# Block transposes on VectorE and 32x32 score tiles in the paged attention of a decoder step

## The chip, the cores and the metric

One NeuronCore of a Trainium2 chip runs the whole program. The metric is the device time of one launch in microseconds (us), as the median of several runs. The core has TensorE (PE, matmuls), VectorE (DVE), ScalarE (ACT), GpSimd (POOL) and SyncE (SP, which here only issues DMAs), and sixteen DMA engines that they share. Each engine works through its own queue in order and waits on semaphores. SBUF and PSUM have 128 partitions; PSUM has eight banks of 512 f32 columns.

## What is computed

One inference step of a hybrid decoder layer: a prompt of 1024 tokens and eight samples of eight new tokens each, with shared weights. The part that the change touches is the samples' attention over a paged cache. Each sample has eight pages of 128 past keys and values; a page of keys is 128 x (8 heads x 128) f32, 512 KB, of values the same. Each head's 128 channels are two components of 64, and the two softmaxes are subtracted.

```python
def sample_attention(q, k_new, v_new, lam, k_cache, v_cache, page_table, layer):
    k_past = k_cache[layer, page_table].reshape(b, -1, N_HEADS, 2, HEAD_DIM)
    v_past = v_cache[layer, page_table].reshape(b, -1, N_HEADS, V_DIM)
    s_past = jnp.einsum('bqhcd,bkhcd->bhcqk', q, k_past, preferred_element_type=jnp.float32)
    s_new = jnp.einsum('bqhcd,bkhcd->bhcqk', q, k_new, preferred_element_type=jnp.float32)
    s_new = jnp.where(jnp.tril(jnp.ones((t, t), dtype=bool)), s_new, NEG)
    s = jnp.concatenate([s_past, s_new], axis=-1) * scale
    p = diff_probs(s, lam).astype(v_new.dtype)      # softmax of component 0 - lam * softmax of component 1
    return (jnp.einsum('bhqk,bkhe->bqhe', p[..., :n_past], v_past)
            + jnp.einsum('bhqk,bkhe->bqhe', p[..., n_past:], v_new))
```

Around it stand the input projection (q, k, v, a pooling input u and two gates), prompt attention, a pooling mixer, the merge of both branches and a gated channel mixer.

## The kernel before

The program has five phases, each engine's part written out by hand in one function per phase (`pe_phase2`, `act_phase2` and so on), with counted semaphores between. Nothing is scheduled by a tool: the order of the code is the order on each engine.

**Phase 1** projects q, k and v head by head and does the prompt's attention of head h beside the projection of head h+1. `pe_head` has nine steps s; a step has scores (`pe_scores`, L338), a projection piece, transposes of the probabilities (`pe_probs_transpose`, L351) and the values. VectorE's part is `dve_head`: in step s first `dve_probs` of step s-1 (L672 to L675), then `dve_max` (L663 to L665), and in step 1 also the scaling L656. The last head has no next projection; in its place stand nine **chunks** (`pe_chunk`, L1011) of the gates' projection. A chunk is one 128-column weight tile against 384 (or, the last of three, 320) tokens, 8 x 3 matmuls, since each product is split in three for precision. There are 14 weight tiles, 42 chunks.

**Phase 2** is the paged part. It goes in 32 turns of two key pages, and five more for the values that lag behind. Per key page TensorE makes eight 128x128 transposes into two PSUM banks (`pe_key_page`, L1068), ScalarE copies them out (`act_key_page`, L1181, `ktp`), and `pe_page_scores` (L1083) makes eight matmuls: the 32 stationary columns of a head are its 8 queries x 2 components beside zeros (`q_blk`, filled by `pool_queries`, L1268), so four heads' results lie in four groups of 32 partitions. `pe_new_scores` (L1093) does the same for the new keys. When a sample's eight pages are done, `dve_keys` takes the maximum, `act_sample_exp` the exponentials (`es`), and `dve_keys` makes the matrix `pick_r`, with which `pe_probs` (L1101, L1107) transposes, normalises and subtracts the probabilities in one matmul per page. `dve_pages` (L1246, L1248) copies them to SBUF (`pts`), and `pe_value_page` (L1126) multiplies them with the values (`v_pg`), five turns later. In nearly every turn stands one of the remaining 33 chunks.

Keys have a ring of four pages (`RK`), values one of five (`RV`); the last two value pages go to key slots. SP loads them page by page (`sp_load_page`, L1296), reading the page's number from SBUF first, in one queue with the weight tiles (`fm_load`, L1470, one raw buffer, waits until POOL has split the tile before). Gate results of the first six tiles stay in SBUF (`sig_p`), the other eight go to DRAM from a ring of two rows (`act_spill`, L1036) and come back in phase 3. Before phase 2's first keys SP does this, in order:

```python
            for g in range(2):
                sp_load_keys(e, g)
            sp_store_kv(e, NH - 1, 1)
            e.wait_ge(b7_free, b_use(NH - 2, True, ("o", TT - 1)) + 1)
            e.wait_ge(kv_st[0], NH // 2 * 64 + 1)
            for g in range(2, RK):
                sp_load_keys(e, g)
```

`sp_store_kv` waits for the last head's keys to have their gain (POOL, L781), since they share SBUF with it. `phase1_over` waits until the last head's outputs are stored.

## Time and profile before

| | us |
|---|---|
| median of 3 runs | 2083.44 |
| lowest, highest | 2081.55, 2084.08 |
| profiled execution: its span | 2081.0 |
| phase 2, first key transpose (551.0) to last value page (825.2) | 274.2 |
| TensorE busy | 2073.9 |
| VectorE, ScalarE, GpSimd busy | 1045.5, 677.1, 493.4 |

A row of the timeline has the start, the duration, the engine, the source line, the operation with what it writes and reads, and how many instructions were merged. Matmuls are pipelined: a row's duration holds the pipe's end, so what a piece costs is read from its start to the next one's start. An f32 matmul shows as two records.

### The profile page before, as it was taken

What the parts mean: (1) busy time and instruction counts of PE and PEld (TensorE: products, weight loads), DVE (VectorE), ACT (ScalarE), POOL (GpSimd) and SP (SyncE); (2) the same over time, 40 slices, a digit from 0 to 9 for tenths busy, and PEclk for the clock granted to TensorE, in tenths of its full rate; (3) what the DMA queues carried; (4) which work ended last, traced back from release to release, by engine and by line L of the source; (5) the groups of instructions that cost most, each with busy time, mean ns of one, the idle gap of its engine ahead of it and who ended that gap; (6) DMA issues with size and microseconds to landing.
All of it is one profiled execution on the core that took longest, in us unless ns stands there. A gap on an engine that the chain in (4) does not pass through costs nothing.

```text
span 2081.0 us, 34047 instructions
## 1 busy us (share of the span) xinstructions
PE 2073.9 (100%) x13497; PEld 1904.7 (92%) x13497; DVE 1045.5 (50%) x1400; ACT 677.1 (33%) x1328; POOL 493.4 (24%) x358
## 2 busy tenths in 40 slices
PE   9999999999999999999999999999999999999999
PEld 8888888888898998999999989999899999899997
DVE  6766666665311111466553433555555455555556
ACT  5444445444444442225112322221131122113120
POOL 5333333332111011332322011221221122022110
PEclk9999999999999999999999999999999999999999
DMA  5222212122388887212224500110111111112112
GB/s 152 58 63 58 62 41 57 32 63 78 102 269 274 309 302 246 59 37 68 83 90 135 166 11 31 51 46 28 53 60 32 42 51 42 32 53 60 32 41 98
DMA packets 174545, 185.53 MB, mean 89 GB/s; under 512 B 8240, under 2 KB 147260, under 8 KB 174404
## 3 DMA queue, kind: packets, MB, share of 16 engines
q1 hardware_dynamic: 162588, 174.10, 26.8%
q10 hardware_dynamic: 11824, 9.51, 1.4%
q8 instruction: 102, 1.67, 0.3%
q14 instruction: 31, 0.25, 0.0%
HBM read 160.57 MB, written 23.24 MB: 88 GB/s over the span
## 4 chain that ended last, share of the span: by engine, by line
PE 99%; DVE 0%; ACT 0%; issue 0%; POOL 0%; POOLq 0%; DVEq 0%
PE PS L1498 39%; PE PS L2260 13%; PE PS L1011 8%; PE PS L2015 5%; PE PS L282 4%; PE PS L284 4%; PE PS L283 4%; PE PS L338 4%; PE PS L362 3%; PE PS L1068 3%; PE PS L351 2%; PE PS L1083 2%; PE PS L1126 2%; PE PS L1519 1%; PE PS L1531 1%; PE PS L317 1%
## 5 line engine op out<-in xcount | busy, mean ns | idle before, releaser
L1485 POOL TENSOR_TENSOR fw_lo<-fw_raw,fw_hi 128x1024 fp32r<-128x1024 f32 x86 | 215.9, 2510 | 876.5 <-ACT fw_hi L1481 876.5
L1498 PE MATMUL PS<-m_hi,fw_hi 128*128 128x384 f32 (+1 forms) x1032 | 228.2, 329 | 0.0
L1498 PE MATMUL PS<-m_lo,fw_hi 128*128 128x384 f32 (+1 forms) x1032 | 227.5, 328 | 0.0
L1498 PE MATMUL PS<-m_hi,fw_lo 128*128 128x384 f32 (+1 forms) x1032 | 227.4, 328 | 0.0
L2388 DVE TENSOR_TENSOR x<-x,PS 128x512 f32<-128x512 f32 x198 | 136.2, 688 | 142.2 <-PE PS L2260 142.0
L1498 PEld LDWEIGHTS PS<-m_hi,fw_lo 128*128 128x128 f32 x1032 | 176.3, 188 | 0.0
L1498 PEld LDWEIGHTS PS<-m_lo,fw_hi 128*128 128x128 f32 x1032 | 176.3, 188 | 0.0
L1498 PEld LDWEIGHTS PS<-m_hi,fw_hi 128*128 128x128 f32 x1032 | 176.0, 188 | 0.2
L282 PE MATMUL PS<-w_hi,act_hi 128*128 128x384 f32 (+1 forms) x456 | 164.7, 361 | 0.0
L284 PE MATMUL PS<-w_hi,act_lo 128*128 128x384 f32 (+1 forms) x456 | 153.6, 337 | 0.0
L283 PE MATMUL PS<-w_lo,act_hi 128*128 128x384 f32 (+1 forms) x456 | 153.1, 336 | 0.0
L2260 PE MATMUL PS<-wd_hi,f_hi 128*128 128x512 f32 x360 | 143.8, 399 | 0.1
L2260 PE MATMUL PS<-wd_lo,f_hi 128*128 128x512 f32 x360 | 142.0, 394 | 0.0
L1481 ACT ACTIVATE fw_hi<-fw_raw 128x1024 fp32r<-128x1024 f32 x86 | 91.3, 1061 | 150.1 <-DMA fw_raw<-in_w_up_dram 73.2
L2260 PE MATMUL PS<-wd_hi,f_lo 128*128 128x512 f32 x320 | 126.2, 395 | 0.0
L1011 PE MATMUL PS<-act_hi,fw_hi 128*128 128x384 f32 (+1 forms) x336 | 114.1, 340 | 0.0
L1181 ACT ACTIVATE ktp<-PS 128x512 f32<-128x512 f32 x128 | 69.6, 596 | 133.8 <-PE PS L1068 133.8
L1011 PE MATMUL PS<-act_hi,fw_lo 128*128 128x384 f32 (+1 forms) x336 | 109.7, 327 | 0.0
L1011 PE MATMUL PS<-act_lo,fw_hi 128*128 128x384 f32 (+1 forms) x336 | 109.6, 326 | 0.0
L2309 ACT ACTIVATE f_c<-f_c 128x1104 f32<-128x1104 f32 x22 | 24.6, 1120 | 255.2 <-DVE f_c L2362 255.1
L496 ACT ACTIVATE E<-PS,negm 128x256 f32<-128x256 f32 (+7 forms) x128 | 93.8, 740 | 26.4 <-DVE negm L665 25.4
L282 PEld LDWEIGHTS PS<-w_hi,act_hi 128*128 128x128 f32 (+1 forms) x456 | 85.3, 187 | 14.7 <-ACT raw L468 5.8
(317 smaller groups left out, 4254.7 us busy)
## 6 DMA issues: line engine op xcount, KB each, us to landing
k_pg<-in_cache_k_dram SPq DMA_DIRECT2D x64, 512.0 KB, 5.0
v_pg<-in_cache_v_dram SPq DMA_DIRECT2D x62, 512.0 KB, 5.2
fw_raw<-in_w_up_dram SPq DMA_DIRECT2D x44, 512.0 KB, 4.0
fw_raw<-in_w_in_dram SPq DMA_DIRECT2D x24, 512.0 KB, 4.5
wd_raw<-in_w_down_dram SPq DMA_DIRECT2D x22, 512.0 KB, 4.7
w_raw<-in_w_in_dram SPq DMA_DIRECT2D x21, 512.0 KB, 5.3
out_dram<-raw SPq DMA_DIRECT2D x16, 512.0 KB, 3.8
ga_scratch<-ga_ring ACTq DMA_DIRECT2D x8, 544.0 KB, 7.1
```

What stands on the lines that cost most here:

```text
L282: e.matmul(out, a_hi, h3, start=kt == 0, stop=False)
L283: e.matmul(out, a_hi, l3, start=False, stop=False)
L284: ins = e.matmul(out, a_lo, h3, start=False, stop=s < QT and kt == KT - 1)
L338: ins = e.matmul(PS[:, 2 * c + b // 512, 0:w], qT[slot][c * HD:(c + 1) * HD, s * P:(s + 1) * P], kT[slot][c * HD:(c + 1) * HD, b:b + w], s ...
L496: ins = e.activation(E[s % 2][:, c, 0:n], scores_ps[:, c, 0:n], ACT.Exp, bias=negm[:, s % 2, c:c + 1], scale=SCALE, accum_out=den[:, s % 2 ...
L1011: ins = e.matmul(PS[:, PJ + use % 2, 0:cw], w[n % 2][:, kt, :], x[:, kt, c0:c0 + cw], start=first and kt == 0, stop=last and kt == KT - 1)
L1481: e.activation(fw_hi[slot][:, 0:kts, :], fw_raw[:, 0:kts, :], ACT.Copy).then_inc(fw_head, 1)
L1485: e.tensor_tensor(fw_lo[slot][:, 0:kts, :], fw_raw[:, 0:kts, :], fw_hi[slot][:, 0:kts, :].bitcast(F32), ALU.subtract).then_inc(fw_tail, 1)
L1498: ins = e.matmul(PS[:, 3 * slot + c, 0:cw], w[slot][:, kt, :], x[:, kt, c0:c0 + cw], start=first and kt == 0, stop=last and kt == KT - 1)
L2015: ins = e.matmul(wo_banks(t)[:, half, :], a, w[:, half * 512:(half + 1) * 512], start=start, stop=stop)
L2260: ins = e.matmul(PS[:, bank, :], a, w[:, half * 512:(half + 1) * 512], start=first and k == 0, stop=last and k == 1)
L2388: ins = e.tensor_tensor(v, v, PS[:, bank, :], ALU.add)
```

## The change

Keys are no longer transposed by TensorE. A page lands in `k_ring`, one tensor of twelve slots, and VectorE transposes it in place in 32x32 blocks (`dve_turn_keys`): the channels of a block then lie in the 32 partitions that held its keys. Scores contract over 32 channels at a time. The queries must therefore lie in all four partition groups: SP writes them to DRAM (`q_dram`) and reads them back four times (`sp_load_queries`), and POOL spreads them in `q_blk` for one sample at a time. A sample's scores are one block of work, 32 matmuls of 64 columns for the new keys and 128 of 256 columns for the eight pages, each on one of 16 tiles of 32x32. Row group i writes bank i, four channel blocks and two heads of a pair accumulate. The columns come out in another order, which `act_sample_exp` puts right. VectorE sums the new scores over four banks first.

TensorE then has per sample: scores, two chunks, probabilities, four value pages, a chunk, four value pages and the new values, a chunk. One chunk stands ahead of the first sample. The last sample's values go to freed key slots. `es` has one buffer. Of the gate results only four tiles stay (`SIG_KEPT`); ten go to DRAM from one row `ga_row` in three pieces each, and two of them come back to `sig_p` at the start of phase 3. Seven key pages fit ahead of phase 2's memory (`KEYS_EARLY`), and VectorE turns six of them in the last head of phase 1.

```diff
@@ dve_head
+                if not proj and 1 <= s <= KEYS_TURNED_EARLY:
+                    dve_turn_keys(e, s - 1)
@@ memory
+        SIG_KEPT = 4
+        KEY_GROUP = NPG // 2
+        RK = 3 * KEY_GROUP
+        KEYS_EARLY = (raw_at[1] - R3 - SIG_KEPT * fit(TOK)) // fit(NH * VD)
+        KEYS_TURNED_EARLY = KEYS_EARLY // 2 * 2
+        k_ld = [sem(f"k_ld{j}") for j in range(RK // 2)]
@@ TensorE
+            e.wait_ge(k_turned, (b + 1) * NPG)
+            for r in range(2):
+                for x in range(XB):
+                    for i in range(4):
+                        part = slice(i * QB, (i + 1) * QB)
+                        for g in range(HG):
+                            c = (2 * g + r) * VD + x * QB
+                            ins = e.matmul(PS[g * QB:(g + 1) * QB, B_S + i, 0:2 * P], queries(g, r, x, part),
+                                           pages[part, :, :, c:c + QB], start=r == 0 and x == 0, stop=r == 1 and x == XB - 1)
+            ins.then_inc(sc_full, 1)
@@ pe_phase2
+            pe_chunk(e, P_FIRST, {})
+            for b in range(NB):
+                fill = [lambda p=p: pe_chunk(e, p, {}) for p in chunks_of(b)]
+                pe_scores_of_sample(e, b)
+                fill[0]()
+                fill[1]()
+                pe_probs(e, b)
+                for j in range(KEY_GROUP):
                     pe_value_page(e, b, j)
+                fill[2]()
+                for j in range(KEY_GROUP, NPG + 1):
+                    pe_value_page(e, b, j)
+                fill[3]()
@@ VectorE
+        def dve_turn_keys(e, g):
+
+            e.wait_ge(k_ld[g % RK // 2], 32 * (g // RK + 1))
+            page = k_ring[:, g % RK, :]
+            e.transpose(page, page).then_inc(k_turned, 1)
@@ SP
-            for g in range(2, RK):
+            for g in range(KEYS_EARLY):
                 sp_load_keys(e, g)
+            e.wait_ge(b7_free, b_use(NH - 1, False, ("k", 2)) + 1)
+            for b in range(NB):
+                e.dma_start(q_dram[:, b, :, :], qT_s[:, :, b * NS:(b + 1) * NS]).then_inc(q_st, 16)
+            e.wait_ge(q_st, 16 * NB)
+            for b in range(2):
+                sp_load_queries(e, b)
             for p in range(TT):
                 sp_chunk(e, p)
+            phase1_over(e)
+            sp_load_keys(e, KEYS_EARLY)
+            for g in range(2, RV):
+                sp_load_values(e, g)
+            for g in range(KEYS_EARLY + 1, RK):
+                sp_load_keys(e, g)
@@ SP, per sample
+                e.wait_ge(sc_full, b + 1)
+                for g in range(RK + b * NPG, RK + b * NPG + KEY_GROUP):
...
+                for k in range(NPG):
+                    if k == KEY_GROUP:
+                        sp_chunk(e, fill[2])
+                    if b * NPG + k + RV < (NB - 1) * NPG:
+                        sp_load_values(e, b * NPG + k + RV)
```

TensorE before, in a turn of phase 2 (a chunk stands ahead of these rows and behind them): transposes of a key page to PSUM, scores of the page before it from `ktp`, two value pages, scores, the next transposes.

```order
L1068 MATMUL PS<-ident,k_pg_103 128x128 x8
L1083 MATMUL PS<-ktp_113,q_blk_106 32x128 x4
L1083 MATMUL PS<-ktp_114,q_blk_106 32x128 x4
L1126 MATMUL PS<-v_pg_108,pts_121 16x256 x4
L1126 MATMUL PS<-v_pg_109,pts_121 16x256 x4
L1083 MATMUL PS<-ktp_115,q_blk_106 32x128 x4
L1083 MATMUL PS<-ktp_116,q_blk_106 32x128 x4
L1068 MATMUL PS<-ident,k_pg_104 128x128 x8
```

TensorE now, in the first sample: all scores in one piece (the first two rows), and after two chunks the probabilities with four value pages right behind them.

```order
L1089 MATMUL PS<-kT_s_53,q_blk_107 32x64 x32
L1098 MATMUL PS<-k_ring_102,q_blk_107 32x256 x128
...
L1106 MATMUL PS<-pick_r0_103,es_112 128x64 x8
L1112 MATMUL PS<-pick_r0_103,es_112 128x64
L1131 MATMUL PS<-v_pg0_123,pts0_113 16x256 x4
L1131 MATMUL PS<-v_pg1_124,pts0_113 16x256 x4
L1131 MATMUL PS<-v_pg2_108,pts0_113 16x256 x4
L1131 MATMUL PS<-v_pg3_109,pts0_113 16x256 x4
```

The transposes are gone from TensorE, and no chunk stands between a sample's probabilities and its values any more.

VectorE before, in step 1 of phase 1's last head: the end of `dve_max`, the scaling, and the four instructions of step 1's probabilities.

```order
L665 TENSOR_SCALAR negm_63<-row_max_62 128x2
L656 TENSOR_TENSOR raw1_81<-raw1_81,rs_61 128x3x256
L672 RECIPROCAL rden_65<-den_64 128x2
L673 TENSOR_SCALAR E1_87<-E1_87,rden_65 128x256
L674 TENSOR_SCALAR rden_65<-rden_65,neglam_66 128x1
L675 SCALAR_TENSOR_TENSOR E1_87<-E1_87,rden_65 128x256
```

VectorE now, at the same place.

```order
L665 TENSOR_SCALAR negm_63<-row_max_62 128x2
L656 TENSOR_TENSOR raw1_81<-raw1_81,rs_61 128x3x256
L1227 STREAM_TRANSPOSE k_ring_102<-k_ring_102 128x1024
L672 RECIPROCAL rden_65<-den_64 128x2
L673 TENSOR_SCALAR E1_87<-E1_87,rden_65 128x256
L674 TENSOR_SCALAR rden_65<-rden_65,neglam_66 128x1
```

The turn of the first key page, with its wait for the page's load, stands ahead of the step's probabilities; five more follow, one in each of the next steps.

## Rows read from the trace of the kernel before

**Rows 1.** The page: busy time of each engine, and the chain by engine.
```profile
PE 2073.9 (100%) x13497; PEld 1904.7 (92%) x13497; DVE 1045.5 (50%) x1400; ACT 677.1 (33%) x1328; POOL 493.4 (24%) x358
...
PE 99%; DVE 0%; ACT 0%; issue 0%; POOL 0%; POOLq 0%; DVEq 0%
```

**Rows 2.** Phase 2: window, PE, PEld, DVE, ACT, POOL busy, clock, DMA share, GB/s.
```profile
551.00:825.40 274.40, 274.40 (x3180) 245.46 (x3178) 33.05 (x93) 108.13 (x211) 30.61 (x39) 1.00 0.83 278
679.00:711.00 32.00, 32.00 (x385) 28.70 (x384) 3.23 (x10) 11.99 (x23) 2.86 (x3) 1.00 0.93 322
676.00:684.00 8.00, 8.00 (x95) 7.02 (x94) 1.69 (x8) 4.14 (x10) 0.00 (x0) 1.00 0.99 378
```

**Rows 3.** Timeline of TensorE in phase 2: start, duration, engine, line, what, records.
```profile
638.52 0.39 PE L1011 MATMUL PS<-act_hi,fw_hi 128*128 128x320 f32 x1
...
642.12 1.04 PE L1068 MATMUL PS<-ident,k_pg 128*128 128x128 f32 x8
643.09 0.65 PE L1083 MATMUL PS<-ktp,q_blk 128*32 128x128 f32 x16
...
643.77 1.05 PE L1126 MATMUL PS<-v_pg,pts 128*16 128x256 f32 x16
644.63 0.62 PE L1083 MATMUL PS<-ktp,q_blk 128*32 128x128 f32 x16
...
646.03 0.42 PE L1011 MATMUL PS<-act_hi,fw_hi 128*128 128x384 f32 x1
...
650.28 1.04 PE L1068 MATMUL PS<-ident,k_pg 128*128 128x128 f32 x8
...
654.48 1.90 PE L1101 MATMUL PS<-pick_r,es 128*128 128x64 f32 x16
...
656.41 0.42 PE L1011 MATMUL PS<-act_hi,fw_hi 128*128 128x384 f32 x1
```

**Rows 4.** Timeline of TensorE, last head: scores on two row halves.
```profile
528.32 1.78 PE L338 MATMUL PS<-kT,qT 64*128 64x512 f32 x8
```

**Rows 5.** The new keys' scores of one sample: duration, first and last start.
```profile
L1093 PE MATMUL PS<-kT_s,q_blk x16: 219/219/219, 643.5 to 643.7; 128*32 128x64 f32 x16
```

**Rows 6.** Timelines of VectorE, SP and TensorE early in the last head.
```profile
498.24 0.95 DVE L656 TENSOR_TENSOR raw<-raw,rs 128x768 f32<-128x768 f32 x1
...
503.37 0.68 SPq L881 DMA_DIRECT2D out_dram<-raw  x1
505.53 1.51 SPq L1296 DMA_DIRECT2D k_pg<-in_cache_k_dram  x2
...
503.40 0.38 PE L351 MATMUL PS<-ident,E 128*128 128x128 f32 x2
```

**Rows 7.** DMA to landing: two keys from 505.5, last outputs (551.6), eight spills.
```profile
DMA to landing us min/median/max: 3.7/4.2/4.7
...
DMA to landing us min/median/max: 2.3/2.3/2.3
...
DMA to landing us min/median/max: 2.7/7.1/8.0
```

**Rows 8.** Timeline of the last sample, from maximum to copied probabilities.
```profile
805.80 1.23 DVE L1230 TENSOR_REDUCE smax<-PS 128x1 f32<-128x1024 f32 x1 [0.65 <-PE PS L1083]
...
809.85 0.25 DVE L1241 TENSOR_SCALAR pick_r<-pick,sden 128x64 f32<-128x64 f32 x1
...
812.97 0.39 PE L1107 MATMUL PS<-pick_r,es 128*128 128x64 f32 x2
...
813.78 0.21 DVE L1248 COPY pts<-PS 128x64 f32<-128x64 f32 x1
```

**Rows 9.** Timeline of TensorE at the program's start.
```profile
8.35 1.91 PE L255 MATMUL PS<-ident,xt 128*128 128x128 f32 x8
...
11.03 0.52 PE L301 MATMUL PS<-w_hi,act_hi 128*128 128x384 f32 x1
...
13.46 0.33 PE L301 MATMUL PS<-w_hi,act_hi 128*128 128x384 f32 x1
```

More of the change, by code:

```diff
@@ L1088, in pe_new_scores, with key_groups @@
[L1088 to L1095 removed]
+        def key_groups(b):
+            first, second = 2 * b % 3, (2 * b + 1) % 3
+            return min(first, second), max(first, second), first > second
@@ L1786, in dve_phase3 @@
             e.tensor_copy(pre[:, 4 * P:4 * P + 3 * P // 2], PS[:, 7, PREP7:PREP7 + 3 * P // 2]).then_inc(prep_done, 1)
[L1787 to L1788 removed]
+            for c in range(NC):
+                e.wait_ge(ga_st[c], 16 * N_SPILLED)
             for m in range(KT):
```

370 lines of the change are left out of this document (154 added, 216 removed).

## The prediction

> **What bounds the kernel now.** I read three views in this order. The page's busy shares and its chain come first: TensorE is busy for 2073.9 of 2081.0 us and 99% of the chain is its own work [rows 1]. So a microsecond leaves the time only if TensorE issues less, and every new wait of TensorE adds in full. The windows come second [rows 2]: the paged part of the program (first key page at 551.0, last value page at about 825.2) takes 274.2 us, with the DMA engines 83% busy on average, 93% over 32 us in its middle, and 99% at 378 GB/s at their fullest. The second resource is therefore close behind the first. The third is TensorE's timeline inside that part [rows 3], which gives what each piece takes from its start to the start of the next.
>
> From [rows 3]: eight key transposes of a page 0.97 us (642.12 to 643.09); a page's eight score matmuls and the new keys' scores 0.68 (to 643.77), of which the new ones are 0.22 [rows 5]; two value pages 0.86 (to 644.63), so 0.43 each; scores and transposes of one more page 1.40 (to 646.03); the nine probability matmuls 1.93 (654.48 to 656.41); a projection chunk 4.25 at 384 columns (646.03 to 650.28) and 3.60 at 320 (638.52 to 642.12). Check: a key page is (0.97 + 0.46 + 1.40) / 2 = 1.42 and 64 are 91; new scores 2, 72 value pages 31, probabilities 15.5, and 33 chunks x 4.03 = 133 make 272.5 against 274.2.
>
> **The change part by part.**
>
> 1. TensorE's key work goes. Per sample that is 8 x 1.42 + 0.2 = 11.6 us. In its place stand 32 matmuls of 64 columns and 128 of 256 columns, each two records in the trace (before, a page's eight score matmuls show as x16 [rows 3]). Now tiles. Four column tiles run side by side before: 16 records of two value pages at 256 columns take 0.86 us, 4 x 0.215 [rows 3], so a record streams for 0.215 us and four share it. Two row tiles do as well: of the eight records of 64-row scores at 528.32, each half of the rows has two of 512 and two of 384 columns, 2 x (0.43 + 0.32) = 1.5 us, and all eight take 1.78 with the pipe's end [rows 4]; the halves in turn would take 3.0. Sixteen tiles are not in the trace. If all run side by side, 256 records / 16 x 0.215 = 3.45 us. If only two row tiles do, 6.9; if rows go in turn, 13.8. Issuing is no bound: sixteen records start within 0.2 us [rows 5], 14 ns each, so 16 in 0.22, a stream's length. I take 3.45, plus 0.45 for the new scores' 64 records at the closest issue seen and 0.2 for the change of tiling: 4.1 us per sample. Saved: 7.5 us x 8 = 60.
>
> The page "TensorE: Matmul & The Clock Gate" of the Trainium skill (section "Wait — 56ns, not 53.3ns?") speaks against this: starts never come closer than about 25 ns. By it the sum would have 256 x 25 ns = 6.4 us, an estimate that brings the forecast to about 2078. The row has 14 ns, so I go by the row. The same page's part 3 gives 10.6 times for sixteen tiles.
>
> 2. VectorE gets 64 block transposes of 1024 elements. No such row exists. VectorE's plain rate: 768 elements take 0.95 us, a 1024-element reduction 1.23 [rows 6, 8]. I take 1.2 us; the bounds are 0.6 (two elements at once) and 2.2 (half rate). Eight are 9.6 us. They start when the probabilities are copied, and TensorE meanwhile has nine value pages 3.9, two chunks 8.1 and the new scores 0.45: 12.4 us. They are hidden up to 1.55 us each. If that cover goes, each further 0.1 us costs 0.8 per sample.
>
> The page "Vector Engine (DVE) Microarchitecture Reference" (section 3.8) says that the transpose sustains one element per cycle and lane, an estimate of 1.07 us; no run here shows it.
>
> 3. ScalarE loses the copies of the transposed keys, two a page. It was busy for 108 of 274 us [rows 2] and held TensorE up nowhere, so this is worth nothing.
>
> 4. The probabilities now stand directly before the values; a chunk stood between before. TensorE waits for both copies: they end at 813.99, where its next piece could start at about 813.15, 0.19 after the last record of L1107 as at 656.22 to 656.41 [rows 8]. That is 0.9 us per sample. The chain before it (maximum, exponentials, sums, picking: 805.80 to 810.10) is 4.3 us [rows 8], with one more small addition and one longer reduction about 5; two chunks, 8.1 us, cover it.
>
> TensorE's own sum per sample: 4 chunks 16.1, scores 4.1, probabilities 1.95, wait 0.9, values 3.9: 27.0 us. Before it was 34.3.
>
> 5. **DMA sets a floor under this.** A sample moves 16 pages of 0.524 MB, 4/3 of a weight tile (0.7 MB) and 4/3 of a spilled row (0.74 MB): 9.8 MB. At 378 GB/s [rows 2] that is 26.0 us; at the 93% that 32 us of before reached, 28.0. The order of the loads adds to it. Keys are asked for when the scores are done; a first page needs 3.7 us to land [rows 7] and each further one 1.39 (0.524 MB at 378 GB/s), so eight land 13.4 us later, with two thirds of the weights and spills about 15.8. Values wait for free slots (a ring of five, released only from 11.3 us on) and behind those: pages five to seven land at about 17.2, 18.6 and 20.0, and are wanted at 17.5, 17.9 and 18.4. So a wait of about 1.6 us: 28.6 us per sample for six samples, and 27.0 for the last two, which load less. The deeper key ring moves keys ahead, but not this.
>
> 6. **The start of the part.** Page 7 doesn't fit in the early ring and is asked for once the last head's outputs are stored: those are sent 0.6 after the head ends and need 2.3 us [rows 7], so with reading the page's number the load goes out about 3.7 after the end, lands 3.7 later, and pages 6 and 7 are turned by 9.8. TensorE has one chunk and the new scores until 4.7: it waits 5.1 us.
>
> Paged part: 4.25 + 5.1 + 6 x 28.6 + 2 x 27.0 = 235 us. Against 274.2: -39.
>
> 7. **A new wait in the last head.** VectorE is to turn page 0 right after step 1's scaling, at 499.2. But the key loads stand on SP behind the storing of the last head's keys and values (until 504.05) and go out from 505.53; the second starts about 1.1 later and lands after 4.7, at 511.4 [rows 6, 7], and the semaphore counts pages in pairs. VectorE is queued behind it with its probabilities of step 1, which TensorE needs at 503.40 [rows 6]. So: 511.4 + 1.2 + 1.3 for the four probability instructions = 513.9, and TensorE waits 10.5 us. The five later turns fall in VectorE's waits for ScalarE's exponentials; the page has it idle half the time [rows 1], and I count them at nothing; without that cover they would cost 1.2 each. After so long a stop I expect the lower clock: at the program's start a record of 384 columns took 0.52 us at 11.03 and 0.33 at 13.46 [rows 9]; 2.4 GHz came some 5 us after the steady work began at 8.35, and until then half the speed is lost, so up to 2.5 us; I take 2, and 1.5 for the wait of step 6.
>
> 8. The queries go out to DRAM and back, with a wait on SP between. The key transposes of the last head, for which SP waits, move from 505.5 to about 516; sixteen small DMAs of some 0.5 us each and two landings of 3 follow, and POOL splits the third weight tile only behind the queries, at about 535; chunk 6 wants it at about 540. Nothing, but with little to spare: up to 5 us in the range. The two gate rows that are reloaded in the next part cost 3 us of idle DMA time. The spill through one row waits for a store three chunks old; that took 7.1 us [rows 7] and has about 12.
>
> **Sum**, on the profiled execution: 2081.0 - 39 + 10.5 + 2 + 1.5 = 2056. The median of the runs is 2.4 above that span, so 2058.
>
> **The rivals.**
>
> - *The block transposes run at half rate (2.2 us).* Then VectorE sets the period: 8 x 2.2 + scores 3.5 + two chunks 8.1 + probabilities and copies 3.0 + handing over 0.3 = 32.5 us; the part takes 4.25 + 7 + 8 x 32.5 - 5 = about 266, and the total is 2083.4 - 8 + 14 = about 2090, slower. It decides from 1.55 us, and the gain is gone at about 2.1. For it: no row of such an instruction on 4-byte data. Against it: every 4-byte row of VectorE runs at about one element per ns.
> - *Row tiles share something.* Two at a time: 3.45 more per sample, of which the DMA wait gives back some: about 2077. One at a time: 10.3 more, about 2130. Against it are the two row tiles of [rows 4]; four are not shown.
> - *DMA comes later than I count* (weights and key loads stuck behind each other on SP): 31 us per sample for six, 14 more, about 2072.
> - *DMA hides wholly*: 27.0 throughout, about 2048.
> - *It doesn't do what it says*: if VectorE's key wait in the last head were absent, 12 less; I see no reason for that.
>
> **How the numbers follow.** Forecast 0.48, DMA hidden 0.15, DMA late 0.12, two row tiles at a time 0.08, half-rate transposes 0.12, rows in turn 0.05. The range 2040 to 2084 holds the first four. A measurement of this kernel tells 0.2%, 4 us, from no change. Faster than that are the first four less their upper edges, 0.77; slower are the last two, 0.16; 0.07 remain.
>
> **What would show it.** The transposes' mean (1.2 us). The 256 score records of a sample within about 3.7 us. One wait of VectorE on a key load near 499 to 511, and one of TensorE of 10 us near 503. A TensorE wait of about 5 us before the first sample's scores, of 0.9 after each sample's probabilities, and small ones on value loads. DMA above 90% through the middle of the part. I am wrong if TensorE waits before most samples' scores, if the score block takes 7 us or more, or if value waits exceed 3 us each.

## The result and the profile after

The changed kernel takes 2116.2 us (2114.4 to 2117.4) against 2082.5 (2080.8 to 2084.1): 1.0164 times the time before, interval 1.0152 to 1.0176. The forecast was 2058, with 2084 as its upper end; it is slower by 1.6% where a gain of 1.2% was forecast. The profiled execution has a span of 2114.1 us.

TensorE's waits from 480 us to the end of phase 2 (engine, line, released by; total us, times, longest). Before, the same view is empty.
```profile
PE PS L1131 <- DMA v_pg<-in_cache_v_dram: 24.8, 20, 4.7
PE PS L351 <- DVE E L675: 10.5, 1, 10.5
PE PS L1131 <- DVE pts L1221: 5.5, 8, 0.7
PE PS L1098 <- DVE k_ring L1227: 4.6, 1, 4.6
PE PS L1098 <- issue: 3.0, 5, 0.8
PE PS L1016 <- issue: 2.7, 1, 2.7
```
The second row is the forecast wait in the last head, 10.5 us to the tenth. The fourth is the wait for key pages 6 and 7 (forecast 5.1), the third that for the copied probabilities (forecast 0.9 a sample; 0.69 here, and some 0.3 inside the row before it). The first row was forecast at 9.6, and the last two, in which TensorE waits for nothing that the profile knows, not at all.

Windows as in [rows 2]: phase 2 as a whole, then three stretches of the second sample.
```profile
563.46:854.54 291.08, 250.30 (x4052) 199.55 (x4050) 97.97 (x158) 39.52 (x82) 33.09 (x55) 0.93 0.75 261
624.30:637.80 13.50, 8.96 (x83) 7.05 (x82) 9.86 (x10) 0.98 (x2) 0.00 (x0) 1.00 0.98 333
637.90:644.60 6.70, 5.48 (x38) 2.32 (x39) 0.00 (x0) 0.38 (x1) 0.00 (x0) 0.50 0.99 343
644.80:662.90 18.10, 17.50 (x388) 15.58 (x388) 3.06 (x10) 3.41 (x7) 3.12 (x5) 1.00 0.50 169
```
The part takes 291.1 us, and one projection chunk more stands behind its last value page. The DMA engines are 75% busy, less than before. The clock, 1.00 throughout before, is 0.93: in the wait that begins at 633.95 it falls (at 637.9) to 0.50, the lower of the two levels, and stays there for 6.8 us.

TensorE's timeline of that sample, projection rows left out, and SP's beside it.
```profile
609.45 0.80 PE L1089 MATMUL PS<-kT_s,q_blk 32*32 32x64 f32 x60
...
610.10 2.77 PE L1098 MATMUL PS<-k_ring,q_blk 32*32 32x256 f32 x132
613.64 2.70 PE L1098 MATMUL PS<-k_ring,q_blk 32*32 32x256 f32 x122 [0.76 <-issue]
616.27 0.42 PE L1016 MATMUL PS<-act_hi,fw_hi 128*128 128x320 f32 x1
...
627.11 1.92 PE L1131 MATMUL PS<-v_pg,pts 128*16 128x256 f32 x32 [0.69 <-DVE pts L1221]
...
633.32 0.63 PE L1131 MATMUL PS<-v_pg,pts 128*16 128x256 f32 x8
638.65 1.05 PE L1131 MATMUL PS<-v_pg,pts 128*16 128x256 f32 x8 [4.70 <-DMA v_pg<-in_cache_v_dram]
639.95 1.05 PE L1131 MATMUL PS<-v_pg,pts 128*16 128x256 f32 x8 [0.24 <-DMA v_pg<-in_cache_v_dram]
```
```profile
617.10 4.00 SPq L1271 DMA_DIRECT2D k_ring<-in_cache_k_dram  x4
624.20 0.39 SPq L1460 DMA_DIRECT2D fw_raw<-in_w_in_dram  x1
624.64 2.08 SPq L1287 DMA_DIRECT2D q_c<-q_scratch  x4
627.47 3.93 SPq L1271 DMA_DIRECT2D k_ring<-in_cache_k_dram  x4
632.17 1.44 SPq L1271 DMA_DIRECT2D v_pg<-in_cache_v_dram  x2
```
Two things are to be seen. The block of scores takes 6.8 us from its first start (609.45) to the chunk behind it (616.27), of which 0.76 is a stop, where 4.1 was forecast. And the first refilled value page is asked for at 632.17, 15 us behind the first key page: four key pages, a weight tile that can't go before POOL has split the last (until 624.2), four query DMAs and four key pages are ahead of it on SP. It lands 6.4 us later and was wanted at 633.6.

VectorE's block transposes are as forecast (1.2 us), and TensorE waits for them only in the last head and ahead of the first sample. VectorE's own idle time before them, 24.7 us, is waiting for key pages:
```profile
L1227 DVE STREAM_TRANSPOSE k_ring<-k_ring 128x1024 f32<-128x1024 f32 x64 | 73.6, 1212 | 24.7 <-DMA k_ring<-in_cache_k_dram 24.7
```

The forecast's sum beside the trace, in us. The pieces are summed over the eight samples, each from its first start to the next piece's, with the waits taken out; the 5.9 are the 5.7 of the view above and two stops too short for it. The last row of "after" runs to the end of the chunk that stands behind the last value page.

| Term | forecast | after |
|---|---|---|
| phase 2 begins later by | 12.5 | 12.4 |
| 33 chunks | 133.1 | 140.0 |
| eight blocks of scores | 32.8 | 51.2 |
| probabilities, values | 15.6, 31.2 | 16.9, 45.8 |
| waits for copies, for pages 6 and 7 | 7.2, 5.1 | 5.5, 4.6 |
| waits for value pages | 9.6 | 24.8 |
| stops without a cause in the profile | 0 | 5.9 |
| lower clock | 1.5 | in the rows above |
| phase 2 | 236 | 295 |

### The profile page after: what moved, and what is told of

Read it like the earlier page. It is cut to its first block, busy times and chain, and to the rows that moved or that the text cites. A ratio compares the mean times of both kernels' runs of the same rounds, so it can differ in the third digit from the quotient of the medians.

```text
span 2114.1 us, 35690 instructions
## 1 busy us (share of the span) xinstructions
PE 2055.5 (97%) x14393; PEld 1863.8 (88%) x14393; DVE 1117.7 (53%) x1471; ACT 608.3 (29%) x1200; POOL 496.7 (23%) x373
## 4 chain that ended last, share of the span: by engine, by line
PE 93%; DMA 3%; SPq 2%; DVE 1%; issue 1%; POOL 0%; ACT 0%; POOLq 0%; DVEq 0%
PE PS L1488 39%; PE PS L2255 13%; PE PS L1016 6%; PE PS L2010 4%; PE PS L282 4%; PE PS L284 4%; PE PS L283 4%; PE PS L338 3%; PE PS L362 3%; DMA v_pg<-in_cache_v_dram 2%; PE PS L1098 2%; PE PS L351 2%; PE PS L1131 1%; PE PS L1509 1%; PE PS L1521 1%
## 5 line engine op out<-in xcount | busy, mean ns | idle before, releaser
L2347 DVE COPY st_col<-f_ext 128x2 f32<-128x2 f32 x44 | 7.8, 177 | 178.0 <-ACT f_ext L2322 178.0
L496 ACT ACTIVATE E<-PS,negm 128x256 f32<-128x256 f32 (+7 forms) x128 | 93.6, 739 | 24.8 <-DVE negm L665 23.7
```

Source lines behind the costliest of these rows:

```text
L496: ins = e.activation(E[s % 2][:, c, 0:n], scores_ps[:, c, 0:n], ACT.Exp, bias=negm[:, s % 2, c:c + 1], scale=SCALE, accum_out=den[:, s % 2 ...
```

## The experiments

**The order on SP, and the turns in the last head.** In e1 SP issues the next queries and the second four key pages behind the eight value loads. In e2 VectorE turns its six early pages in steps 3 to 8. e4 has both.

```diff
@@ e1, sp_phase2, per sample
-                if b + 2 < NB:
-                    e.wait_ge(qb_ready, b + 1)
-                    sp_load_queries(e, b + 2)
-                for g in range(RK + b * NPG + KEY_GROUP, RK + (b + 1) * NPG):
-                    if g < NB * NPG:
-                        sp_load_keys(e, g)
...
                     if b * NPG + k + RV < (NB - 1) * NPG:
                         sp_load_values(e, b * NPG + k + RV)
+                if b + 2 < NB:
+                    e.wait_ge(qb_ready, b + 1)
+                    sp_load_queries(e, b + 2)
+                for g in range(RK + b * NPG + KEY_GROUP, RK + (b + 1) * NPG):
+                    if g < NB * NPG:
+                        sp_load_keys(e, g)
@@ e2, dve_head
-                if not proj and 1 <= s <= KEYS_TURNED_EARLY:
-                    dve_turn_keys(e, s - 1)
+                if not proj and 3 <= s <= 2 + KEYS_TURNED_EARLY:
+                    dve_turn_keys(e, s - 3)
```

> The changed kernel, but on SP the loads of a sample's second four key pages and of the next queries stand behind its eight value loads instead of ahead of them. Theory A (the value pages come late because SP issues them behind keys that are needed much later, and each stop lowers TensorE's clock): TensorE's waits for value loads fall from 24.8 us to under 6, the low-clock stretches in the paged part mostly go, and a sample's period falls from 38 to about 31 us: some 40 us less in all, about 2076. Rival (the DMA engines simply can't carry more): waits move to the key pages or stay, the period stays at 36 or more, and the total changes by less than 10 us.

> The changed kernel, but the six early key turns of VectorE stand in steps 3 to 8 of the last head instead of 1 to 6, when the pages have landed. If the wait of 10.5 us in step 2 and the low clock after it (0.5 from 508.2 to 518.4) are what the last head loses, the total falls by 10.5 + about 2.3, to about 2103, and the paged part starts at 551 again. Rival: the wait moves to another step, or the third weight tile's splitting comes late instead, and less than 6 us is gained.

> Both edits of the first two runs. If they are independent, their gains add: about 2063 by theory A. If the earlier start of the paged part runs into DMA that isn't ready, less than 8 us of the second edit's gain is kept.

Measured: e1 2110.7 (1.0138, interval 1.0113 to 1.0164), e2 2109.4 (1.0135, 1.0118 to 1.0152), e4 2104.3 (1.0115, 1.0098 to 1.0132). TensorE's waits in e1:
```profile
PE PS L1098 <- issue: 16.0, 7, 3.8
PE PS L351 <- DVE E L675: 10.6, 1, 10.6
PE PS L1131 <- DMA v_pg<-in_cache_v_dram: 10.5, 12, 2.2
```
The order on SP did hold the values up: their waits fall from 24.8 to 10.5. But the stops rise from 5.7 us (3.0 and 2.7) to 17.7 (16.0 and 1.7), and most of the gain is gone: 5.5 us less where 40 were expected. In e2 the 10.5 us wait goes, and half of it comes back: 4.3 us of TensorE waiting for ScalarE's copies and 1.4 for a weight tile, of which below; phase 2 begins at 557.5 and not at 551. In e4 the two gains add: 5.5 and 6.8 alone, 11.9 together. The runs of one kernel lie 2 to 11 us apart (e1 from 2104 to 2115), so between neighbours the waits in the profile say more than the times.

**What the score block is bound by.** e3 makes each 256-column matmul as two of 128, in two passes, so 512 records a sample; e5 leaves out the second half, so 256 records of 128 columns (on the kernel of e4).

```diff
@@ e3, pe_scores_of_sample
-            for r in range(2):
+            for half in range(2):
+              for r in range(2):
...
-                            ins = e.matmul(PS[g * QB:(g + 1) * QB, B_S + i, 0:2 * P], queries(g, r, x, part),
-                                           pages[part, :, :, c:c + QB], start=r == 0 and x == 0, stop=r == 1 and x == XB - 1)
+                            ins = e.matmul(PS[g * QB:(g + 1) * QB, B_S + i, half * P:(half + 1) * P], queries(g, r, x, part),
+                                           pages[part, half, :, c:c + QB], start=r == 0 and x == 0, stop=r == 1 and x == XB - 1)
@@ e5, the same place
+                            ins = e.matmul(PS[g * QB:(g + 1) * QB, B_S + i, 0:P], queries(g, r, x, part),
+                                           pages[part, 0, :, c:c + QB], start=r == 0 and x == 0, stop=r == 1 and x == XB - 1)
```

> The changed kernel, but each score matmul of 256 columns is made as two of 128, in two passes over the same tiles: twice the records, the same columns. A sample's past scores take 6.2 us now for 256 records. Theory of issue (some 17 ns per record, plus short stops): 512 records take 11 to 13 us. Theory of the stream (sixteen tiles are held up by reading or writing columns): the block stays at 6 to 7 us.

> On the kernel of e4. Each of the 256 score records of a sample covers 128 columns instead of 256: the scores of half of each sample's pages are left out, and the output is not the reference's; number of matmuls and of records, and all loads, stay. Theory (the block is bound by how fast TensorE starts records, about 20 ns each on average with the short pauses, not by the 0.215 us for which one streams): a sample's page scores stay at 5 to 6 us, the whole is within 5 us of e4's 2104. Rival (sixteen tiles stream at the rate of the prediction or slower, and the columns set it): page scores fall to half, about 2.7 us, and the time by 8 x 2.7 = 21, to about 2083.

Measured: e3 2174.9, e5 2098.7 (one run each). TensorE in e3, then in e5:
```profile
619.47 1.92 PE L1099 MATMUL PS<-k_ring,q_blk 32*32 32x128 f32 x132
622.80 2.45 PE L1099 MATMUL PS<-k_ring,q_blk 32*32 32x128 f32 x128 [1.41 <-issue]
626.53 2.82 PE L1099 MATMUL PS<-k_ring,q_blk 32*32 32x128 f32 x128 [1.28 <-issue]
629.98 2.77 PE L1099 MATMUL PS<-k_ring,q_blk 32*32 32x128 f32 x122 [0.63 <-issue]
```
```profile
603.73 1.92 PE L1098 MATMUL PS<-k_ring,q_blk 32*32 32x128 f32 x132
610.02 2.77 PE L1098 MATMUL PS<-k_ring,q_blk 32*32 32x128 f32 x122 [4.37 <-issue]
```
A row's duration holds the last record's own time. With that taken off (0.27 us at 128 columns, 0.37 at 256), 132 records of 256 columns start over 2.40 us, 18 ns apart, and 132 of 128 columns over 1.65, 12.5 ns apart. Only the first row of either trace counts for this: the others stand partly or wholly at the lower clock (0.50 from 626.6 to 632.6 in e3). So it is neither the columns alone (they would halve it) nor the starts alone (they would leave it): sixteen tiles take 0.29 us at 256 columns and 0.20 at 128. By an estimate from these two figures that is a stream of 0.18 us for 256 columns (the difference, doubled) and some 0.11 for each group on top; it gives 10 ns a record at 64 columns, and the new keys' records start 10 ns apart. The page "TensorE: Matmul & The Clock Gate" of the Trainium skill (section "Wait — 56ns, not 53.3ns?"), which the prediction weighed, has starts no closer than about 25 ns; these rows have 12.5 and 18, so the rule doesn't hold here. Its sum for the page scores, 6.4 us, missed the 4.7 to 5.2 measured by about as much as my 3.45, on the other side.

The rows show something else too: in e3 there is a stop every 128 records. In e5, where records are used up faster, the stop is longer (4.37 for 2.54 in e4). Its blocks themselves take 40 us instead of e4's 56, but the stops take back 9.6 of that (23.8 against 14.2), and the chunks, more of them at the lower clock, 7: the one run of e5 lies 5.6 us under e4's median, not 21, and 1.9 under e4's profiled execution.

**Are the stops TensorE waiting for its own instructions?** In the trace a queue of instruction fetches (q8) moves packets of 16 KB through the sixteen DMA engines. The changed kernel and the eighteen of the experiments have 142 stops of more than 0.15 us from 480 us to the end of phase 2, and every one of them ends 1.2 to 1.7 us behind the end of such a packet, though in phase 2 two packets begin 3.3 to 23 us apart. That ties the stops to the packets; what makes a packet late is the next question. e6 loads no key pages behind the first twelve, e10 no value pages behind the first five either; waits on the loads left out are lowered to match. Both stand on e4, and TensorE's matmuls are the same in all three.

```diff
@@ e6, sp_phase2, per sample
-                for g in range(RK + b * NPG, RK + b * NPG + KEY_GROUP):
-                    if g < NB * NPG:
-                        sp_load_keys(e, g)
...
-                for g in range(RK + b * NPG + KEY_GROUP, RK + (b + 1) * NPG):
-                    if g < NB * NPG:
-                        sp_load_keys(e, g)
@@ e10, besides
-                    if b * NPG + k + RV < (NB - 1) * NPG:
-                        sp_load_values(e, b * NPG + k + RV)
```

> On the kernel of e4. Only the first twelve key pages are loaded; the 52 later ones are not, and VectorE turns again what lies in the ring (the output is not the reference's). TensorE's and VectorE's instructions stay the same; the core moves 27 MB less in the part. Theory (TensorE's stops inside the score block, 11.6 us in e4 against 2.8 in e2, are waits for its own instructions, which come in 16 KB packets over the same DMA engines and stand behind the key pages): the stops fall to under 3 us, value waits from 10.7 to about 0, and the low clock between with them: about 2104 - 9 - 11 - 6 = 2078. Rival (the stops belong to the block itself, as TensorE can't be fed 320 small matmuls in a row): they stay at about 12, only the value waits go, about 2089. Either way this is the time of TensorE's own work with the new scores, with little of loading in it.

> On the kernel of e6. The value pages behind the first five are not loaded either (the output is not the reference's); only the last sample's eight, the weight tiles, the spilled rows and the queries still move. e6 was no clean test of the theory of e6: value pages still stood in the DMA queues when the score block began, and its stops ended 1.4 to 1.6 us behind the end of a 16 KB packet each time. Theory (TensorE reaches the end of its fetched instructions some 3.4 us into the block, and what is queued at the DMA engines sets how long the next packet takes): with empty queues the stop is 0.3 to 0.8 a sample, 3 to 6 us in all, against 11.5; no value waits and no low clock behind them. The part then takes 4.0 + 4.4 + 8 x (16.1 + 6.4 + 0.6 + 2.1 + 1.0 + 3.9) = 249 us, the span about 2066. Rival (the stops belong to the block): they stay at 11 to 12, the span is about 2073.

Measured, one run each: e6 2095.7, e10 2069.7 with a span of 2067.9. The second block of scores in e4 and in e10, and the transfers of the core from 608.6 to 611.2 in e4 and from 602 to 609 in e10 (queue; packets, MB, share of the engines):
```profile
605.84 2.77 PE L1098 MATMUL PS<-k_ring,q_blk 32*32 32x256 f32 x132
611.15 3.84 PE L1098 MATMUL PS<-k_ring,q_blk 32*32 32x256 f32 x122 [2.54 <-issue]
```
```profile
602.74 2.77 PE L1098 MATMUL PS<-k_ring,q_blk 32*32 32x256 f32 x132
606.20 2.70 PE L1098 MATMUL PS<-k_ring,q_blk 32*32 32x256 f32 x122 [0.69 <-issue]
```
```profile
q1 hardware_dynamic: 290, 1.01, 100.4%
q8 instruction: 1, 0.02, 2.5%
```
```profile
q8 instruction: 2, 0.03, 1.9%
```
The stop stands behind the same record in both. With page loads filling the engines it is 2.54 us; with nothing but instructions moving, 0.69. The packet itself takes as long (1.05 and 1.28 us), but begins 2.9 us behind the first page score in e4 and 0.8 in e10.

e6 missed: 2095.7 where 2078 was expected, stops of 13.7 us all told (under 3 expected) and 8.7 of waits for values (about 0 expected). Value pages were still queued when most blocks began. Its own blocks differ, though, and that is a comparison within one run. The fourth begins with the DMA engines all but idle and has no stop; the fifth begins with page loads moving and stops for 2.37 us (windows as in [rows 2]):
```profile
675.30:678.50 3.20, 3.20 (x172) 2.44 (x157) 0.00 (x0) 0.10 (x1) 0.00 (x0) 1.00 0.02 5
706.10:709.50 3.40, 3.35 (x177) 2.49 (x164) 0.00 (x0) 0.12 (x1) 0.00 (x0) 1.00 0.78 280
```
Idle DMA engines don't make the supply endless. In e3's second sample they are 2% busy while the rows above run:
```profile
622.00:632.60 10.60, 7.89 (x378) 6.09 (x378) 0.00 (x0) 0.00 (x0) 0.00 (x0) 0.58 0.02 5
```
and still the packets begin 3.5 to 3.8 us apart (620.42, 623.90, 627.65, 631.10), with a row of up to 128 records behind each but the last. In none of the twenty kernels do two begin less than 3.26 us apart. So a packet feeds about 128 matmul records with their weight loads (e10's part has 32 packets for 8102 records of both), and a long block is fed no faster than about 27 ns a matmul record, an estimate from 3.5 us and 128, where the tiles themselves could take 12.5 to 18.

In e10 all stops together are 5.2 us, all waits for values are gone, and the part takes what its expectation had summed, 249.1 us:
```profile
558.47:807.61 249.14, 233.97 (x4052) 197.40 (x4050) 97.97 (x158) 39.61 (x82) 33.16 (x55) 0.99 0.29 88
```
With the same chunk behind it, that is 253 us of work and handing over against 295 in the changed kernel. 42 us are what loading costs it: 24.8 of waits, 12.7 in the value pages and 3.7 in the chunks, and 0.7 of stops. The 16.4 in the middle are mostly the lower clock behind the waits: it holds for 41.0 us of phase 2 in the changed kernel, 34.4 of them with TensorE at work, and for 6.8 in e10; half of the difference is 14. The other 2 are not told apart; the ends of the matmul pipe, one for each wait, would be of that size.

**Spreading the block.** If TensorE outruns its instructions, pauses in the dense block should let them catch up. In e7 the second half of the scores stands in the middle of the next chunk; in e14 the block is in four pieces of 64 records, each behind 1.5 to 2.5 us of chunk (`pe_first_scores` makes the new keys' scores and the first piece).

```diff
@@ e14, pe_phase2 (on e11; added lines alone)
+            pe_first_scores(e, 0)
             for b in range(NB):
+                pe_page_scores(e, b, 0, (2, 3))
+                pe_chunk(e, chunks_of(b)[0], {3: lambda: pe_page_scores(e, b, 1, (0, 1)),
+                                              6: lambda: pe_page_scores(e, b, 1, (2, 3))})
...
+                pe_chunk(e, chunks_of(b)[3], {3: lambda: pe_first_scores(e, b + 1)} if b + 1 < NB else {})
```

> On the kernel of e4. The second half of a sample's page scores (r = 1) stands in the middle of the first chunk, behind 12 of its 24 matmuls, instead of right behind the first half. Nothing is added or left out. Theory (TensorE uses up the instructions it has fetched within the dense block): the 2 us of few instructions in the middle let the next ones arrive; the stops go from 11.6 to under 4 us; against it stand two more changes between small and full tiles a sample, 0.1 to 0.2 each, 2 us: about 2104 - 8 + 2 = 2098. Rival (the stops have to do with entering the block, whatever its length): each half has its own, they stay or double, and the time is 2106 to 2116.

> On the kernel of e11. A sample's page scores are issued in four pieces of 64 records, each behind 1.5 to 2.5 us of projection matmuls: the first (with the new keys' scores) inside the last chunk of the sample before, the second behind that chunk, the third and fourth inside the first chunk. Nothing is added or left out. Theory (the stops, 11.3 us in e11, are the end of the fetched instructions, with the next packet queued behind page loads): with pieces this short the packets have time, stops fall under 3 us, the low clock behind them with them; against it some 0.3 us a sample for more changes of tiling: 2094 - 9 - 3 + 2 = 2084. Rival (the stops only move to other places, since the page loads are queued all the time and every packet comes 3 to 4 us late wherever it is wanted): stops of 8 to 12 in the chunks, 2090 to 2096.

Measured: e7 2099.2 (1.0081, 1.0064 to 1.0098), e14 2088.0 (1.0034, 1.0021 to 1.0046). Waits in e14:
```profile
PE PS L1135 <- DMA v_pg<-in_cache_v_dram: 11.0, 14, 3.0
PE PS L1135 <- DVE pts L1227: 5.5, 8, 0.7
PE PS L1101 <- DVE k_ring L1233: 4.9, 1, 4.9
PE PS L351 <- ACT PTs L490: 3.0, 1, 3.0
...
PE PS L1101 <- issue: 0.4, 2, 0.2
```
e14 has every page load of e4, its part runs with the DMA engines at 82% instead of 79%, and the stops are 0.4 us instead of 14.2, or of 11.3 in e11, from which e14 differs in nothing but the cut of the block. That is the theory's result for the stops (the time is 4 us above its 2084), and the rival's (late packets wherever they stand) is out for this order of work. It is not out for all: e15 to e19 below have the same four pieces, and stops from 1.1 to 12.1 us. Between the two, e7 reached its time (2099.2, 2098 expected) with stops of 9.1 us, where under 4 were expected, 5.7 of them now in the chunk.

**Waits given back.** e8 puts the first four value pages into the third chunk, to cover VectorE's copies; e13 does so with both groups of value pages, on e12; e15 does it on e14.

```diff
@@ e8 (added lines alone, here and below)
+                pe_chunk(e, chunks_of(b)[2], {3: first_values})
@@ e13 (e15 with 2 for 3)
+                pe_chunk(e, chunks_of(b)[2], {3: lambda: values(0, KEY_GROUP)})
+                pe_chunk(e, chunks_of(b)[3], {3: lambda: values(KEY_GROUP, NPG + 1)})
```

> On the kernel of e4. The third chunk of a sample starts right behind the probabilities, and the first four value pages stand behind 9 of its 24 matmuls (1.5 us) instead of right behind the probabilities. Theory: VectorE's two copies (TensorE's wait of about 1 us a sample, 7.8 in all) are covered, value pages are wanted 1.5 us later for the first four, so value waits shrink too, by 0 to 4; about 2104 - 8 - 2 = 2094. Rival (the waits are one chain: pages five to eight wait for slots that the first four free 1.5 us later, while they are wanted at the same distance from the scores): the microsecond saved at the copies comes back as a wait on the sixth or seventh page, about 2102 to 2106.

> On the kernel of e12. A sample's first four value pages stand behind 9 of the 24 matmuls of its third chunk, and the other five behind 9 of the 24 of its fourth, so that the two groups stay a whole chunk apart, which e8 gave up (there the slots of pages one to three were freed 1.5 us later for the same demand, and the waits on values doubled). Theory: VectorE's two copies are covered (7.8 us), values are wanted 1.5 us later with the same distance for their slots, so value waits fall by 1 a sample at most: about 2089 - 8 - 3 = 2078. Rival (value pages come as DMA can bring them, and what is saved at the copies comes back as waits on values): 2086 to 2090.

> On the kernel of e14. The first four value pages stand behind 6 of the 24 matmuls of the third chunk, and the other five behind 6 of the fourth, so VectorE's copies are covered by 1 us of the third chunk. Theory: TensorE's eight waits for the copies (5.5 us, and 2.4 for an empty pipe) go: 6 to 8 less than e14, about 2077, below the kernel before. Rival (values come at the rate of the DMA engines, and what is saved returns as value waits, as 4 of 8 did in e13): 2080 to 2084.

Measured: e8 2120.7 (1.0188), e13 2105.2 (1.0109), e15 2089.4 (1.0034). The wait for the copies went in all three, and came back elsewhere. e8 is 16 us slower than e4: value waits rose from 10.5 to 20.0, where a slot had 2.7 us instead of 4.3 between its release and the next demand, and stops from 14.2 to 17.3. e15 is level with e14: value waits rose from 11.0 to 14.9, stops from 0.4 to 4.2. e13 alone gained, 4.5 us against e12 where 11 were expected: value waits fell from 16.4 to 13.8, and stops rose from 21.3 to 23.8.

e12 puts two chunks ahead of the first sample and three in the last, to cover the wait for pages 6 and 7; e17 does it with the scores in four pieces; e18 also moves the second group of values 1.5 us on.

> On the kernel of e11. Two projection chunks stand before the first sample's scores instead of one, and the last sample has three instead of four. Theory (the wait for pages 6 and 7 of the first sample, 4.5 us, is covered by the second chunk; the last sample loads nothing that needs the fourth): about 4.2 less than e11, 2089. Rival (DMA sets the start: what the second chunk covers is only moved to the first sample's value pages, which are wanted at the same time as before): 0 to 1 less, 2092 to 2093.

> On the kernel of e16. The edit of e12 again: two chunks before the first sample's scores, three in the last sample. In e12 the wait of 4.5 us went, but the block of scores then stood in the queue of page loads, with stops of 17.8 us, and the time rose. With the block in four pieces (theory) the stops stay under 2 us and the gain shows: e16 less 4, about 2081. Rival (the chunk is also missing at the last sample, or the earlier demand for values returns as waits, as DMA sets this stretch): e16 less 0 to 1.

> On the kernel of e17. Value pages five to eight and the new one stand inside the fourth chunk behind 9 of its 24 matmuls instead of before it; the next sample's first scores behind 18. From the first four pages' release of their slots to the demand for the refilled ones there are 5.8 us instead of 4.3. Theory (the wait on values, 11.0 us in e14, is this distance against the 5 to 6 us that a page takes in a full queue): it falls to 3 or less, e17 less 7, about 2074, below the kernel before. Rival (pages come at the engines' rate and the later release moves the next ones back by as much): less 0 to 3.

Measured: e12 2109.7 (1.0137), e17 2090.1 (1.0044), e18 2093.2 (1.0056), against 2094.5 of e11 and 2085.4 of e16. The 4.5 us wait became 0.2 to 0.4 each time. In e12 the stops rose from 11.3 to 21.3, in e17 from 1.1 to 6.0 and the longest value wait from 2.5 to 6.5. In e18 the value waits fell from 16.5 to 7.5, where 3 or less were expected, and the stops rose from 6.0 to 12.1. All three missed.

**The last head.** In e4, e7 and e14 TensorE still waits there for ScalarE (3.0 to 4.4 us) and, before e11, for a weight tile (1.7). e11 lets POOL split the tile ahead of the queries, e16 lets SP load it ahead of them.

```diff
@@ e11, pool_phase2
+            for p in range(NC):
+                pool_chunk(e, p)
             step(e.memset(q_blk[:, :, :, :], 0.0))
             pool_queries(e, 0)
@@ e16, sp_phase2
+            for p in range(2 * NC):
+                sp_chunk(e, p)
             e.wait_ge(b7_free, b_use(NH - 1, False, ("k", 2)) + 1)
             for b in range(NB):
                 e.dma_start(q_dram[:, b, :, :], qT_s[:, :, b * NS:(b + 1) * NS]).then_inc(q_st, 16)
```

> On the kernel of e7. In the last head POOL splits the weight tile of chunk 6 before it clears and fills the query block, instead of behind it. Theory (the queries' way through DRAM holds up POOL, and chunk 6 waits for its weights, 1.7 us, and ScalarE behind it with the probabilities, 3.6 us): both waits of TensorE go, 5.3 us, and about 1 us of low clock: 2099 - 6 = 2093. Rival (the tile itself is loaded late, as SP makes the queries' sixteen DMAs first): the wait stays, 2099.

> On the kernel of e14. SP loads the weight tile of chunks 9 to 11 before it sends the queries to DRAM and fetches them back, instead of behind. In e14 this load leaves at 527.7 us and lands at 531.4; ScalarE waits 5.2 us for it, and TensorE 3.0 for ScalarE's copies of the probabilities queued behind. Theory (the queries' way through DRAM, step 8 of the prediction, costs the last head these 3 us in all versions with the late turns): TensorE's wait in the last head goes, 2088 - 3 = 2085. Rival (the tile's buffer is not free much earlier, or the queries arrive later and POOL holds the next tile): 2087 to 2088.

Measured: e11 2094.5 (1.0053, 1.0037 to 1.0070), e16 2085.4 (1.0013, 1.0003 to 1.0022). ScalarE and SP in e14, ahead of e16's edit:
```profile
531.46 1.06 ACT L1479 ACTIVATE fw_hi<-fw_raw 128x1024 fp32r<-128x1024 f32 x1 [5.21 <-DMA fw_raw<-in_w_in_dram]
```
```profile
522.92 4.71 SPq L1295 DMA_DIRECT2D q_c<-q_scratch  x8
527.67 0.43 SPq L1468 DMA_DIRECT2D fw_raw<-in_w_in_dram  x1
```
The tile leaves behind the eight query loads, and ScalarE, in order, keeps TensorE's probabilities waiting behind it. In e11 the 1.7 went and 3.5 of the wait for ScalarE stayed; in e16 TensorE has no wait left from 480 us to phase 2, which begins at 551.4, as in the kernel before. Both causes named were right, one engine each.

**One place of SP's order alone.** e19 (on e16) issues four of the last sample's value pages behind the seventh's own.

> On the kernel of e16. In the seventh sample SP issues the first four value pages of the last sample (which go into free key slots) behind the seventh's own value pages instead of ahead of them. In e16 the seventh sample's period is 36.0 us against 32.2 to 35.4 of the others, and its TensorE waits 2.5 us for value page five (3.5 for the three), as four pages of nobody's present need are ahead in the queue; 3.4 us of low clock follow. Theory (it is the order of issue on SP that makes value pages late): 3.5 of waiting and 1.5 of low clock go, 2085.4 - 5 = 2080.5, level with the kernel before (2082.5) or just below. Rival (what is left is the engines' rate): 2085, as e16.

Measured: 2086.0 (1.0017, 1.0008 to 1.0026), the same as e16 and not the 2080.5 expected. Two rows of that sample:
```profile
789.69 0.62 PE L1135 MATMUL PS<-v_pg,pts 128*16 128x256 f32 x8 [1.10 <-DMA v_pg<-in_cache_v_dram]
...
797.95 1.11 PE L1101 MATMUL PS<-k_ring,q_blk 32*32 32x256 f32 x17 [2.19 <-issue]
```
The wait for page five fell from 2.5 to 1.1, so the order counts. But the moved loads now stand in the queue when the first piece of scores begins, and it stops for 2.2 us.

No version beats the kernel before. The best, e16, is 0.13% slower (interval 0.03 to 0.22%), about 3 us.

## Why the prediction was wrong, step by step

Right: the transposes on VectorE (step 2, 1.2 us, hidden); the copies' wait (step 4); the wait for pages 6 and 7 (step 6); the last head (step 7), with the wait at 10.5 us and phase 2 at 12.4 us later than before, clock and all. Step 8 was right in its mechanism and was hidden at first: the queries' way cost nothing while TensorE stood still for 10.5 us anyway, and 5 to 6 us as soon as it did not (e2, e4).

**Step 1 failed in its price, and left out a term.** "If all run side by side, 256 records / 16 x 0.215 = 3.45 us", and "Issuing is no bound". All sixteen do run side by side, but a group of sixteen takes 0.29 us, not 0.215: 4.7 to 5.2 us for the page scores, and with the new keys' scores and two changes of tiling 6.1 to 6.5 where 4.1 stood (7.4 in the first sample, part of it at the lower clock). The 14 ns between starts were read on sixteen records in four tiles, which says nothing of a run of hundreds. The 0.45 for the new scores doesn't follow from it either: 64 records at 14 ns are 0.9, and they took 0.65. All this is 18 us in eight samples. The supply of instructions was no term of the sum at all; in the changed kernel it cost 5.9 us, and 14 to 18 once loads had been moved under the block (e4, e1).

**Step 5 failed in its mechanism.** It took the DMA engines' rate for the limit and the values' lateness for 1.6 us a sample. The engines were 75% busy. The limit was the order on SP: its loads stand in one queue with a weight tile that waits for POOL, so the first value page left 15 us behind the first key page. That step had said "Values wait for free slots and behind those", and then priced the queue at the engines' rate rather than by SP's waits. It is 15 us of waits more than forecast, and e1, which changes that order alone, takes 14.3 of the 24.8 away. The rival "DMA comes later than I count" named this cause (weights and key loads stuck behind each other on SP), but priced it at 14 us in all, without the clock.

**What a wait costs was left out.** Seven samples waited for values, and in six of them the clock stood at 0.50 for 3.4 to 6.9 us in and behind the wait, as the forecast had it for the last head, where it was counted once. In phase 2 it was 1.5 us for all; e10 against the changed kernel has 16 us, 14 of it by the granted clock. The waits on values so cost between half and two thirds more than their length.

Together: 18 and 6 for the block, 15 for the waits, 15 for the clock beyond the 1.5 counted, 4 for chunks and other pieces that are dearer even in e10: 59 us before rounding. The list of what would show the forecast wrong named two of these (a block of 7 us, value waits above 3), but no rival held both, and the dearest one (rows in turn) was for another reason. One reading for the rivals was too broad, without consequence: not every 4-byte row of VectorE runs at about one element per ns (L673 takes 0.775 us for 1024).

**What stays open.** That a stop is a wait for a packet rests on all 142 stops, and that page loads make the packet late on e10, on e6's fourth block and on e14; what the fetch waits for within a DMA engine, and what sets the 3.5 us between packets when the engines are idle, no run shows. Why e17 and e18 have 6 and 12 us of stops where e16 has 1.1, with the same four pieces, was not told apart from what else moved. Whether a deeper value ring would take the last 11 to 14 us of value waits wasn't tried.

## What to carry over

Count instructions, not only work: a block with a matmul record every 20 ns (320 in 6.4 us) where one every 56 stood (208 in 11.6) must also be fed, through the same DMA engines as the data, so spread it between sparse work instead of issuing it in one piece. Price a load from the moment its queue reaches it, with every wait ahead of it on the issuing engine, and only then by bandwidth. And where TensorE has never waited, price its new waits above their length: here 24.8 us of them cost 14 to 16 more, by the lower clock behind them.

## What was unexpected in the hardware

- Sixteen 32x32 tiles of f32, 256 columns: 18 ns from start to start, 0.29 us a group; 128 columns 12.5 ns, 0.20 us.
- TensorE's instructions come in 16 KB packets of about 128 matmul records (64 f32 matmuls) with their weight loads, in dense blocks 3.5 us apart, at the closest 3.3. Denser work stops at the end of a packet: in blocks of 320 records for 0.2 to 0.7 us with no page loads queued (e10), up to 4.4 with them (e5); in blocks of 576 for up to 1.8 us with the DMA engines idle (e3).
- The granted clock of phase 2 was 0.93 on average with 41 us of waits and stops spread over it, and 0.99 with 15 (e10), for the same matmuls on TensorE.
